# One shared room from retention to sample attention, with loads issued a stage earlier

## What is computed

```python
z = rms(x) * (1 + scale) + shift            # scale, shift, gates: rows of silu(c) @ w_ada + b_ada
p = z @ w_in                                # 3072 columns: q, k, v of 8 attention heads; q, k, v, g of 4 retention heads
att = dilated_window_attention(rope(q), rope(k), v)   # prompt: its own keys; sample: 2048 cached keys and values per sequence
ret = retention(rotate(q), rotate(k), v, state)       # chunks of 128; sample: a state per sequence is read and updated
mix = concat(att, silu(g) * group_norm(ret) * gain)
x = x + gate_a * (mix @ w_out)
x = x + gate_f * (square(relu(norm(x) @ w_ff1)) @ w_ff2)     # hidden width 4096
y = rms(x) * (1 + scale_l) + shift_l
```

## Time and profile before

| | |
|---|---|
| median of 3 runs | 1843.76 us (1841.23 to 1846.09) |
| the profiled execution's own time | 1834.07 us |
| its span, first to last instruction | 1832.3 us |
| busy: PE, DVE, ACT, POOL | 1547.5, 810.8, 401.2, 506.7 us |
| DMA | 185.40 MB, mean 101 GB/s |

### The profile page before, as it was taken

The page is one execution under the profiler, slowest core; times in us unless marked ns, Lnnn a source line. Parts: engine busy times, 40 slices in busy tenths (PEclk is TensorE's granted clock), DMA queues, the critical chain, the costliest instruction groups (busy, mean ns, idle before and its releaser), DMA issues.

```text
span 1832.3 us, 22776 instructions
## 1 busy us (share of the span) xinstructions
PE 1547.5 (84%) x8460; PEld 1215.3 (66%) x8460; DVE 810.8 (44%) x1441; ACT 401.2 (22%) x637; POOL 506.7 (28%) x365
## 2 busy tenths in 40 slices
PE   2699999958784844577799999999999999999992
PEld 1577777745553633355587787888878787878882
DVE  5711011006665755222237454544444444454567
ACT  1210111116564210222213211111111111111121
POOL 0200000000101510000035055554444444555536
PEclk7799999978888675788899999999999999999996
DMA  7744443242103217999720211011110111111012
GB/s 297 268 161 159 154 172 120 84 132 65 58 23 99 66 32 195 268 258 260 237 70 24 92 47 46 25 44 46 46 40 28 46 46 46 46 46 46 23 50 83
DMA packets 107308, 185.40 MB, mean 101 GB/s; under 512 B 7241, under 2 KB 57033, under 8 KB 102962
## 3 DMA queue, kind: packets, MB, share of 16 engines
q1 hardware_dynamic: 94978, 161.55, 28.1%
q10 hardware_dynamic: 12272, 23.07, 3.7%
HBM read 160.05 MB, written 24.54 MB: 101 GB/s over the span
## 4 chain that ended last, share of the span: by engine, by line
PE 42%; issue 4%; DVE 2%; POOL 2%; ACT 0%; DMA 0%; POOLq 0%; DVEq 0%; ACTq 0%
PE ps L2220 20%; PE ps L2263 18%; PE ps L2228 2%; PE ps L2194 1%; POOL res L1800 1%; DVE back_r L1718 1%; PE ps L2303 1%; POOL back_zrow L1804 1%; DVE back_r L1717 0%; DVE back_row_f L2127 0%; DVE res L2145 0%; PE ps L2243 0%; POOL back_w_lo L1828 0%; PE ps L2206 0%; DMA back_raw<-in_w_out 0%
## 5 line engine op out<-in xcount | busy, mean ns | idle before, releaser
L1810 POOL TENSOR_TENSOR res<-res,back_row_f 128x512 f32<-128x512 f32 x224 | 309.2, 1417 | 376.1 <-DVE back_row_f L2054 375.2
L2220 PE MATMUL ps<-mix_hi,back_w_hi 128*128 128x512 f32 x512 | 204.3, 399 | 2.4 <-DVE back_w_lo L2043 1.8
L2220 PE MATMUL ps<-mix_hi,back_w_lo 128*128 128x512 f32 x512 | 202.5, 395 | 0.0
L2220 PE MATMUL ps<-mix_lo,back_w_hi 128*128 128x512 f32 x512 | 202.5, 395 | 0.0
L2054 DVE TENSOR_TENSOR back_row_f<-ps,back_gate_f 128x512 f32<-128x512 f32 x224 | 153.3, 690 | 104.6 <-PE ps L2263 102.2
L2263 PE MATMUL ps<-back_w_hi,back_h_hi 128*128 128x512 f32 x448 | 175.9, 393 | 5.5 <-PE ps L2228 5.5
L2263 PE MATMUL ps<-back_w_hi,back_h_lo 128*128 128x512 f32 x448 | 174.4, 389 | 0.0
L2263 PE MATMUL ps<-back_w_lo,back_h_hi 128*128 128x512 f32 x448 | 174.4, 389 | 0.0
L582 PE MATMUL ps<-inp_whi,z_hi 128*128 128x512 f32 x384 | 153.3, 399 | 10.8 <-DVE inp_wlo L542 9.2
L582 PE MATMUL ps<-inp_whi,z_lo 128*128 128x512 f32 x384 | 150.6, 392 | 0.0
L582 PE MATMUL ps<-inp_wlo,z_hi 128*128 128x512 f32 x384 | 150.4, 392 | 0.0
(11 more groups left out here) (334 smaller groups left out, 2629.4 us busy)
## 6 DMA issues: line engine op xcount, KB each, us to landing
back_w_raw<-in_w_ff SPq DMA_DIRECT2D x32, 1024.0 KB, 5.4
inp_room<-in_w_ada SPq DMA_DIRECT2D x16, 1024.0 KB, 5.5
proj<-inp_row ACTq DMA_DIRECT2D x54, 256.0 KB, 2.2
K<-in_cache_k SPq DMA_DIRECT2D x48, 256.0 KB, 12.3
cache_V<-in_cache_v SPq DMA_DIRECT2D x48, 256.0 KB
mod_w<-in_w_ada SPq DMA_DIRECT2D x8, 1024.0 KB, 11.5
x<-in_w_in ACTq DMA_DIRECT2D x16, 512.0 KB, 5.7
inp_room<-in_w_ada_f SPq DMA_DIRECT2D x8, 1024.0 KB, 4.9
```

The source lines that it names most:

```text
L1810: pool.tensor_tensor(dst, dst, row_f[o % 3][:], ALU.add).then_inc(y_added, 1)
L2220: mm = pe.matmul(ps[:, u, :], w[:, k, j * P:(j + 1) * P], z[:, k, rows], start=(k == 0 and a == 0), stop=(k == KT - 1 and a == 2))
```

## The change

All buffers from retention to sample attention are laid by hand into one room of 139 KB per partition (`Room`, `SampleParts`), in which places of a later stage lie beside those of an earlier one.

- Projection: the two halves of the sample rows are added before they are stored (`sample_sum`), so that `proj` holds 64 sample rows; `piece` follows it in VectorE's list.
- Retention rotates in place; at the end of its loads SP issues the sample rows and five tables.
- Sample heads: no low rows and no such addition; the state loads go to ScalarE's queue; SP issues K[0], waits for the first rotation, stores the new keys and values, then issues K[1], V[0], V[1].
- Sample attention: the first two values are there already; VectorE waits for the bias only after pair 0; after the last values SP waits until all keys are turned and loads the first half of w_out into the place of K[1].
- Back: begins with that half loaded; the low part of w1 for group 1 is made after the second square of group 0; `EARLY` is 4, with the other banks opened as they are needed; `root_steps` uses tensor_scalar instead of scalar_tensor_tensor twice; the last shift is done in two halves.

The diff, cut to its core:

```diff
+            def sample_sum(c):
+                n = c % 2 * OUTS + TT
+                dve.wait_ge(s_low, c + 1)
+                dve.tensor_tensor(row[n % ROWS][0:NS, :], ps[0:NS, n % BANKS, :], row[n % ROWS][0:NS, :],
+                                  ALU.add).then_inc(bank_free, 1)
             wait_all(dve, z_ready)
             dve.memset(xs_room[:], 0.0).then_inc(a_zeroed, 1)
             split(0, 0)
-            for i in range(PIECES):
-                split(i, 1)
-                if i:
-                    piece(i - 1)
-                if i + 1 < PIECES:
-                    split(i + 1, 0)
-            piece(PIECES - 1)
+            split(0, 1)
+            for c in range(NCH):
+                sample_sum(c)
+                if c % 2:
+                    piece(c // 2)
+                if c + 2 < NCH:
+                    split((c + 2) // 2, c % 2)
...
+                    rows = P if o < TT else NS
                     act.wait_ge(made, i * 2 * OUTS + n + 1)
                     act.wait_ge(row_free[n % ROWS], i * (16 * 2 * OUTS // ROWS) + 16 * (n // ROWS) + 16)
-                    act.copy(row[n % ROWS][:], ps[:, n % BANKS, :]).then_inc(bank_free, 1)
+                    if o < TT:
+                        act.copy(row[n % ROWS][:], ps[:, n % BANKS, :]).then_inc(bank_free, 1)
+                    else:
+                        act.copy(row[n % ROWS][0:NS, :], ps[NS:P, n % BANKS, :]).then_inc(s_low, 1)
                     act.wait_ge(bank_free, i * 2 * OUTS + n + BANKS + 1)
-                    act.dma_start(out[o * P:(o + 1) * P, ds(i * 2 * CH + s * CH, CH)],
-                                  row[n % ROWS][:]).then_inc(row_free[n % ROWS], 16)
+                    act.dma_start(out[o * P:o * P + rows, ds(i * 2 * CH + s * CH, CH)],
+                                  row[n % ROWS][0:rows, :]).then_inc(row_free[n % ROWS], 16)
...
+class Room:
+    SIZE = 139
+    def __init__(self, nc, ctx):
+        self.nc, self.base = nc, nc.sbuf_base
+        ctx.enter_context(nc.sbuf_tensor("shared_room", [P, self.SIZE * 256], F32))
+    def at(self, name, kb, shape, dt=F32):
+        return self.nc.alloc_sbuf_tensor_at(f"room_{name}", shape, dt, offset=self.base + int(kb * 1024))
+class SampleParts:
+    def __init__(self, nc, ctx, room):
+        self.V = [room.at(f"V{b}", 20 * b, [P, KTILES, AW]) for b in range(2)]
+        self.K = [room.at(f"K{b}", 40 + 20 * b, [P, KTILES, AW]) for b in range(2)]
+        self.q_blocks, self.kT_new = room.at("q_blocks", 80, [P, DB, 4, QCOLS]), room.at("kT_new", 84, [P, 4, NS])
+        self.x = room.at("xs", 85, [NS, IN_W])
+        self.rope = room.at("rope_s", 97, [NS, 2, 2 * H, 8])
+        self.rot = room.at("rot_s", 98, [NS, 2, 2 * RH * RD // 2])
+        self.dmask = room.at("dmask_s", 100, [NS, RH * NS])
+        self.dout = room.at("dout_s", 101, [P, RH, 4, NS])
+        self.din = room.at("din_s", 105, [NS, RH, 4, P])
+        self.gain = room.at("gain", 113, [P, RH * RV])
+        sem = lambda n: ctx.enter_context(nc.semaphore(f"parts_{n}"))
+        self.x_in, self.tables = sem("x_in"), sem("tables")
+        self.k_in, self.v_in = ([sem(f"{n}_in{b}") for b in range(2)] for n in "kv")
+        self.w_out_in = [sem(f"w_out_in{q}") for q in range(4)]
...
+        q_rot, k_rot = ([put(f"{n}{a}", kb + 4 * a, [P, TT, P]) for a in range(2)] for n, kb in (("q", 0), ("k", 8)))
+        q_in, k_in = q_rot, k_rot
...
+            sp.dma_start(parts.x[:], io["proj"][S:S + NS, :]).then_inc(parts.x_in, 16)
+            for dst, n in ((parts.rope[:].rearrange("p a b c -> p (a b c)"), "rope_s"),
+                           (parts.rot[:].rearrange("p a b -> p (a b)"), "rot_s"), (parts.dmask[:], "dmask_s"),
+                           (parts.din[:].rearrange("p a b c -> p (a b c)"), "din_s"),
+                           (parts.dout[:].rearrange("p a b c -> p (a b c)"), "dout_s")):
+                sp.dma_start(dst, io[n]).then_inc(parts.tables, 16)
...
-            sp.dma_start(x[:], io["proj"][S:S + NS, :]).then_inc(x_in, 16)
-            sp.dma_start(lo_rows[:], io["proj"][S + NS:S + P, :]).then_inc(x_in, 16)
-            sp.dma_start(flat4(rope), io["rope_s"]).then_inc(tables, 16)
-            for dst, n in ((flat(rot), "rot_s"), (dmask[:], "dmask_s"), (flat4(dout), "dout_s"), (flat4(din), "din_s")):
-                sp.dma_start(dst, io[n]).then_inc(tables, 16)
-            sp.dma_start(gain[:], io["ret_gain"][0].partition_broadcast(NS)).then_inc(tables, 16)
-            for b in range(2):
-                for q in range(4):
-                    sp.dma_start(state[RD * b:RD * (b + 1), q], st_in[b, :, q]).then_inc(s_in, 16)
-            for b in range(2):
-                load_cached(sp, io, "cache_k", K[b], k_in[b], b)
+            load_cached(sp, io, "cache_k", parts.K[0], parts.k_in[0], 0)
             sp.wait_ge(roped, 1)
             sp.dma_start(io["k_sample"].rearrange("o b t h d -> (o b t) (h d)"), x[:, AW:2 * AW]).then_inc(put, 16)
             sp.dma_start(io["v_sample"].rearrange("o b t h d -> (o b t) (h d)"), x[:, 2 * AW:3 * AW]).then_inc(put, 16)
+            load_cached(sp, io, "cache_k", parts.K[1], parts.k_in[1], 1)
+            for b in range(2):
+                load_cached(sp, io, "cache_v", parts.V[b], parts.v_in[b], b)
...
-            dve.wait_ge(x_in, 32)
-            steps.then(dve.tensor_tensor(x[:], x[:], lo_rows[:], ALU.add))
-            signal(steps, g_ready)
-            dve.wait_ge(tables, 96)
+            dve.wait_ge(parts.x_in, 16)
+            dve.wait_ge(parts.tables, 80)
...
-            act.wait_ge(g_ready, 1)
+            for b in range(2):
+                for q in range(4):
+                    act.dma_start(state[RD * b:RD * (b + 1), q], st_in[b, :, q]).then_inc(s_in, 16)
+            act.wait_ge(parts.x_in, 16)
...
             def values(i, b, first=False):
                 if not first:
                     sp.wait_ge(pv_made, 2 * i + b - 1)
-                load_cached(sp, io, "cache_v", V[b], v_in[b], 2 * i + b)
+                    load_cached(sp, io, "cache_v", V[b], v_in[b], 2 * i + b)
                 sp.dma_start(v_new[b][:], v_put[:, ds(2 * i + b, 1), :]).then_inc(v_in[b], 16)
...
+            sp.wait_ge(turned, 6 * PAIRS)
+            load_w_out(sp, io, raw, parts.w_out_in)
...
             pair(0, first=True)
+            dve.wait_ge(tables, 16)
             with dve.Fori(1, PAIRS) as i:
...
+def load_w_out(sp, io, raw, sems):
+    wv = io["w_out"].rearrange("o (k p) n -> p (o k) n", p=P)
+    for q, sem in enumerate(sems):
+        rows = slice(q * KT // OUT_QUARTERS, (q + 1) * KT // OUT_QUARTERS)
+        sp.dma_start(raw[:, rows, :], wv[:, rows, 0:CH]).then_inc(sem, 16)
...
-    EARLY = len(TAIL_BANKS)
+    ROOM = len(TAIL_BANKS)
+    EARLY = 4
...
-            steps.then(eng.scalar_tensor_tensor(out=col(r1), in0=col(r0), scalar=col(r0), in1=col(v), op0=ALU.mult, op1=ALU.mult))
-            steps.then(eng.scalar_tensor_tensor(out=col(r), in0=col(r1), scalar=-3.0, in1=col(r0), op0=ALU.add, op1=ALU.mult))
+            steps.then(eng.tensor_scalar(col(r1), col(r0), col(r0), col(v), ALU.mult, ALU.mult))
+            steps.then(eng.tensor_scalar(col(r), col(r1), -3.0, col(r0), ALU.add, ALU.mult))
...
-            weights(0)
...
+                a, b = (x[:, t, :], sh_l[:]) if t < TT else (xs[0:NS, :], sh_ls[:])
+                for c in range(2):
+                    cols = slice(c * CH, (c + 1) * CH)
+                    part = pool.tensor_tensor(a[:, cols], a[:, cols], b[:, cols], ALU.add)
+                part.then_inc(l_shifted, 1)
...
-            def hidden(g, s):
+            def hidden(g, s, opening=False):
                 for u in range(MAIN):
+                    if opening and u == 2:
+                        split_w1(1)
...
-            hidden(0, 0)
-            split_w1(1)
+            hidden(0, 0, opening=True)
...
+            def open_bank(m):
                 if m < 3:
                     pe.wait_ge(gated2, OUTS2 * (NG - 2) + m + 1)
+                elif m < ROOM:
+                    pe.wait_ge(sq_done, MAIN * (NG - 1) + m - 2)
                 else:
-                    pe.wait_ge(sq_done, MAIN * (NG - 1) + m - 2)
+                    pe.wait_ge(l_gated, m - ROOM + 1)
+            for m in range(EARLY):
+                open_bank(m)
                 part(*divmod(m, 2), NG - 2)
```

More of the change, by code:

```diff
@@ L897, in group_norm, with stage_prompt_retention @@
     steps.wait()
[L900 removed]
+def stage_prompt_retention(nc, io, ps, ident, mix_hi, mix_lo, room, parts):
     st = Stage(nc, "ret")
@@ L1209, in stage_sample_heads @@
     with st.ctx:
-        x, lo_rows = st.sb("x", [NS, IN_W]), st.sb("lo_rows", [NS, IN_W])
-        rope = st.sb("rope", [NS, 2, 2 * H, 8])
-        rot = st.sb("rot", [NS, 2, 2 * RH * RD // 2])
-        dmask = st.sb("dmask", [NS, RH * NS])
-        dout = st.sb("dout", [P, RH, 4, NS])
-        din = st.sb("din", [NS, RH, 4, P])
-        gain = st.sb("gain", [NS, RH * RV])
-        state = st.sb("state", [P, 4, RH, RV])
```

(42 more changed lines are left out.)

109 lines of the change are left out of this document (46 added, 63 removed).

## The result

The changed kernel took 1793.49 us (median of 4 runs, 1788.25 to 1799.74) beside 1842.49 for the kernel before (4 runs): ratio 0.974, 95% interval 0.9709 to 0.9772. Two further chips gave 1791.52 beside 1844.75 (0.9702, 0.9666 to 0.9738) and 1798.76 beside 1839.55 (0.9768, 0.9725 to 0.9810). The profiled execution took 1794.24 us, its span is 1792.5: 39.8 less than the profiled one of before.

What follows compares the result with a forecast made beforehand. Back-stage groups were taken as bound by matmuls, sample attention by DMA. Terms 2.7 - 5.4 - 18.1 - 3.0 - 1.8 - 5.5 = -31.1 us took the profiled 1834.07 to 1803.0, on the median 1812; range 1798 to 1828 us.

Steps and rivals of the forecast that it cites:

- the same 49 us per group: MLP groups: expected in the changed profile to take the same time per group as before, a term of 0.
- the new addresses cost nothing: Whole kernel: rotating in place and moved buffers keep the same instructions and waits, so no time was counted.
- its two terms: Back stage up to its second group: earlier w_out start, -3.0 us, and no wait for low w1, -1.8 us.
- -18.1: Sample attention: ten loads instead of twelve plus the bias before the last keys, 104.2 us instead of 122.3.
- the term for lost queue time: Sample attention: TensorE's first turn 3.65 us, 1.5 to start and land, 2.6 for pair 1's softmax.
- The rival that gave the stage 9: Sample attention paced by waits, not transfers, each pair leaving a gap: 9 us gained instead of 18.1, 1822 us; chance 10%.
- The bound of -22 for 300 GB/s: Sample attention: the larger gain stated should transfers run at 300 GB/s instead of 272, beside the forecast -18.1.
- Transfers, not the chain: Sample heads: 11.8 MB of transfers, then state stores, set the stage's end near 731, not the chain of small steps; -5.4 us.
- the early parts: Tail: four instead of seven parts ahead of the last products bring the first output 4.0 us earlier, counted as 3.5.
- the small steps: Tail: two 128x1 scalar_tensor_tensor become tensor_scalar and stop waiting for GpSimd's shift; 0.4 us per tile for six tiles.
- The rival by which tensor_scalar waits for GpSimd: Tail: both 128x1 steps stay bound to GpSimd's shifts, so the tail gives 3.5 us, 1815 us in all; chance 8%.
- TensorE's clock would not fall to half in sample attention: Sample attention: the forecast stood against the rival of TensorE at 1.2 GHz, 14 us slower, 1858 us; rival's chance 8%.

Runs made afterwards that it cites:

- a1: Kernel before with the back stage's room 128 bytes further up in SBUF, nothing else moved: 13.3 us faster than before in medians, ratio 0.9917.
- c1: Changed kernel with both first value loads issued in sample attention again, not in the heads: 1804.37 us, 12.9 more than the changed kernel on its chip.
- f2: The changed kernel profiled again, nothing altered, with quick transfers: sample heads 45.7 us, sample attention 132.9 us.
- f1: The kernel before run again, nothing altered, with quick transfers: ratio 0.9994 of before, sample attention 144.0 us.
- e1: Changed kernel with the eight state loads issued by SP ahead of the first key load, not by ScalarE: 1797.69 us, ratio 0.9759 to before.

## Why the prediction was wrong in size

In the profiles the sum was -39.8 us instead of -31.1. The misses, 7.6 in the groups, 3.7 in the opening, 2.4 in the heads and 1.8 in the tail, outweigh the 6.6 that sample attention fell short.

**The step that failed: "the same 49 us per group".** The forecast took "the new addresses cost nothing" as a reason to leave the groups alone. The move took 128 bytes out of the distance between the two operands' buffers, and every matmul of the first product and of w_out starts 5 ns sooner: -7.6 us in the groups, and most of the 3.2 us by which the opening beat what its two terms gave (8.5 - 3.3 - 2.0); a1 shows 7.1 and 2.0 from the 128 bytes alone. The profile of before could have hinted at it: equal shapes at one clock, mostly 396 ns each in the first product and 389 in the second.

**Sample attention, mis-sized: -18.1 became -11.** The mechanism was right, and early values are the whole of it (c1). What was too small is the term for lost queue time: 7.8 us (3.65, 1.5 and 2.6), in which the bias's 2.4 us pass too, beside 4.2 before (122.3 - 118.1), so 1.2 more. The rival that gave the stage 9 named the real cost. The keys of pairs 1 and 2 follow TensorE's turns, and the queue runs dry between them. The first 44 us of the stage in f2, where f1 had a share of 1.00:

```profile
731.60:776.00 44.40, 36.85 (x419) 26.78 (x419) 14.86 (x22) 14.56 (x20) 0.00 (x0) 0.91 0.73 230
```

From the stage's start to the landing of its last keys, f1 and then f2:

```profile
735.10:848.90 113.80, 77.21 (x917) 54.74 (x917) 31.49 (x55) 31.95 (x48) 0.00 (x0) 0.87 1.00 289
```

```profile
731.60:833.40 101.80, 75.33 (x917) 53.74 (x917) 31.59 (x55) 31.86 (x48) 0.00 (x0) 0.92 0.91 271
```

These are 32.9 and 27.6 MB, 107.5 and 90.2 us at 306 GB/s. So 17.3 us of transfers went away (19.3 were counted, at 272 GB/s), and the lost time grew from 6.3 to 11.6, by 5.3 and not by 1.2. That leaves 12.0, and the rest of the stage took 0.9 longer. No wait for pair 1's keys, and a share of 1.06 later on, were right. The bound of -22 for 300 GB/s does not follow from its figures: ten loads of 8.7 us and 7.8 make 95.1, which is 27 under 122.3.

**Heads: -5.4 became -7.8**, mis-sized by the rate. 12.9 MB went through in 43.5 us, 296 GB/s, not 272. "Transfers, not the chain" is half right: the states landed at 17.7 us, the state update ended 35.8 us after the stage's start and not 33.2, and c1 shows the chain alone to take 47.1, where the forecast's terms make 41.6 (33.2, 5.3, 2.4 and 0.7). The late states cost nothing here, as e1 shows.

**Tail: -5.5 became -7.3.** Of the terms, the early parts were right (4.1 to the first output, 3.4 at the end, 3.5 counted); the small steps gave 3.2 and not 2.4, and some 0.7 is left for the halved shifts, counted at -0.1. (2.4 - 1.2 + 1.1 is 2.3; the forecast wrote 2.0.) The rival by which tensor_scalar waits for GpSimd falls (0.21 and 0.27 us inside its operations). The Trainium skill (SBUF — State Buffer, Who interferes with whom) lists tensor_scalar among the operations that can take the port pair shared with GpSimd, under conditions on its operands; these 128x1 ones, at 0.27 and 0.21 us, did not wait.

**Right:** back start (3.3 and 3.6 beside 3.0), low w1 (2.0 beside 1.8), and that TensorE's clock would not fall to half in sample attention (0.87). **Right in part by luck:** projection. Of the +2.8 at retention's start, beside 2.7, projection's end gave 2.0; the other 0.8 came in prompt attention.

**The level.** 1803.0 was forecast for the profiled execution and 1794.2 came; on medians 1812 and 1793.5. Of these 18.5 us, 8.7 are the miss accounted for above, and some 9 are the distance between profiles (39.8) and medians (49.0; 53.2 and 40.8 on the two further chips, where 46 to 50 or about 40, and 46 to 53, were expected). So the terms explain about half of the miss on medians. Pooled, 16 runs of the changed kernel have a mean of 1793.3 and 44 of before 1840.7, 47.4 us apart (43.5 to 51.3, by resampling), while profiles at like levels give 38 to 40. The profiled executions of before (1824 to 1843) lie below its other runs on average; why, stays open. So do 2 us more in prompt attention (188.1 to 189.3, then 189.9 to 192.7), whose code the change does not touch.

## What to carry to other kernels

Before a move of buffers is called free, compute the distance of the two operands of the matmuls that bound the kernel, and compare the durations of equal shapes at one clock: 2.2% of a product's time hung on 128 bytes here. Bytes that are moved out of a transfer-bound stage are worth their transfer time only while something else can fill the queue; look at what the next loads wait for. And where a stage's length hangs on a clock level or a transfer rate that changes by execution, take two or three profiles of either kernel before its difference is read.

## What the runs showed of the hardware

- Matmuls of 128x512 with operands in two buffers: 22.06 us for 96 where the buffers lie a multiple of 256 bytes apart, 22.55 at 128 more, 22.64 at 64 more. The Trainium skill (SBUF — State Buffer, A bandwidth-pool intuition that's wrong) gives TensorE a second, independent read port for weight loads. By that alone one would not expect the place to matter; these runs show that it does, and not by what mechanism. Matmuls of 128x256 showed no such difference (118 to 120 ns from start to start).
- Saturated loads of 2 KB rows ran at 307 GB/s (f1) and 277 in two executions of the kernel before, at 306 (f2) and 269 (the run on a1's chip) in two of the changed one. What sets the rate was not found.
- A 128x1 tensor_scalar runs beside a GpSimd operation on SBUF in 0.21 to 0.27 us; a 128x1 scalar_tensor_tensor waited for its end (0.59 and 1.19 us, beside 0.16 to 0.22 where it met none).
